# Two copies of the recurrence moved to ScalarE, a new entry, and partial sums of the down projection added by GpSimd's DMAs

## The chip, the cores and the metric

The kernel runs on one core of one Trainium2 chip. The metric is the device time of one execution in microseconds, and lower is better. A run's time is that of the whole program; the profile is of one further execution of the same program.

## What is computed

The input is a sequence of 1024 tokens with 1024 channels. Two blocks follow each other, both in float32. The first has a mixture of three branches (a linear recurrence with a 64x64 state per head, a short convolution and a pooling branch), gates and an output projection. The second has windowed attention and retention, then a gated feed-forward network. Cut to what the change touches:

```python
h = rms_norm(x, pre_norm_w)                       # the entry: 1024 x 1024
p = h @ w_in                                      # r, k, v, gates, fills
y_a = rwkv7_branch(...)                           # the recurrence, chunks of 64 tokens
...
m = rms_norm_2(h, ffn_norm_w)
h = h + (silu(m @ w_gate) * (m @ w_up)) @ w_down  # w_down: 2816 x 1024, the down projection
```

## The kernel before, in words

The channels lie on the 128 partitions and the tokens along the free dimension, 1024 of them in two halves of 512 (one PSUM bank each). Matrix products are made with float32r operands split in two: a tile W becomes Whi (a copy rounded to float32r, made by ScalarE) and Wlo = W - Whi (a subtraction by VectorE or GpSimd), and each product is three matmuls: hi x hi, hi x lo, lo x hi. So TensorE's work stands fixed, and the other engines prepare operands and empty banks.

Each engine runs one long program of its own, written as Python generators ("streams"), and the order in which the streams of an engine are woven is written out by hand in `ORDER`: a letter is a stream, a number behind it how many of its steps. An engine takes its instructions strictly in that order; all dependences between engines are semaphores (`S.<signal>.tick(key)` adds, `wait_ge(*S.<signal>.at(key))` waits). `PICKS` says which PSUM bank each product takes where there is a choice. Every engine operation of the same kind has the line of its small wrapper: 120 matmul, 123 transpose, 126 activation, 129 tensor_tensor, 137 scalar_tensor_tensor, 140 copy, 143 memset, 146 DMA. So the profile is read by tiles.

**The entry** (`begin` and `tokens_in`, `token_norms`, lines 658, 1255, 1288, 1825, 1841). ScalarE's queue loads the gain row `pre_norm_w` into one partition of xn[1]. TensorE first makes 4 products of zeros, then spreads the row over 128 partitions by a product with a row of ones, then makes 8 more products of zeros. ScalarE copies the result, times 32, to `g_row`, and after that squares the tokens of each 128-token tile with a running sum. GpSimd raises the sum to the power -0.5, VectorE makes xn = x * rstd * g_row, TensorE transposes it, ScalarE writes Hhi and VectorE Hlo, and the dense products of `w_in` begin.

**The recurrence** (45 to 700 us; stream "s" is `stage`, "i" `invert`, "c" `chain`, "p" `prep`, "g" `group_norm`, "f" and "e" the other consumers of `w_in`). There are 8 units of 512 tokens and 128 channels, each of 8 chunks and 2 heads. For a unit VectorE inverts 32 small triangular matrices `Nn` by 60 dependent operations ("Ntmp" and "Nn"), adds the diagonal, and copies the transposed first half to `Nt` (lines 2060 to 2064; the profile calls it Nn, line 140). SP writes both to memory and reads them back in other layouts for TensorE. The `WU` tile takes two quarters of transposes out of PSUM: rows 0 to 63 by ScalarE, rows 64 to 127 by VectorE (line 2080). Between the small products of the units stand the dense products of `w_in`, which cover their latency. The chain from chunk to chunk goes TensorE, `Xs` on VectorE, TensorE. ScalarE makes `rk`, squares from which a key's norm is had.

**The down projection** (from 2011 us; `down_products` 857, `down` 1764 and 2507, `block_weights` 1777, 2589, 2794 and 3028, `hidden` 1803, 2549 and 2785). The 22 row tiles of `w_down` are paired, and products of 2x2 blocks are made with seven products in place of eight (Winograd's form). 16 blocks w0 to w15 are made: four pairs of output tiles (dp) times four groups of row pairs; a block takes two or three row pairs, and each of its seven products A11, S3, S4, S2, S1, A12, A22 three matmuls per pair. The 16 accumulators `acc` and 4 `x6` lie in SBUF. In group 0 (w0 to w3) ScalarE copies most products there, in the others VectorE adds each product from PSUM to its accumulator:

```python
    def add(to, out, b, name, point):
        dve.wait_ge(*S.dense_pe.at(("prod", name, b)))
        dve.tt(to[:], banks.of(("st", out, b)), to[:], ALU.add).then_inc(*S.ffn_dve.tick((point, b)))
```

VectorE also forms the sums S1 to S4 of the weight quarters (wSrcS), the low halves of S2 to S4 (wLoS), and the sums and low halves of the hidden side (hT). GpSimd makes the low halves of A11, S1, A12 and A22 (wLoA, wLoS) and of three hidden tiles. SP loads a block's weight quarters (wSrcA) after the low halves of the block before have been made: A11 and A21 after S3, S4 and A11, the others after A22.

## Time and profile before

| | |
|---|---|
| time, median of 3 runs | 2244.04 us (2243.98 to 2244.30) |
| the profiled execution | 2244.64 us |
| its span, first to last instruction | 2242.9 us |
| TensorE, VectorE, ScalarE, GpSimd busy | 2218.5, 1554.3, 837.8, 476.1 us |
| first dense product starts | 14.91 us |
| down projection, first and last product | 2011.3 to 2235.6 us |

The windows view gives the busy time of each engine in a stretch of the span; the waits view sums how long an engine, or TensorE's weight loads (PEld), stood idle and what released it; the chain that ended last is followed back from the last instruction; the timeline lists instructions by their start. A matmul's end is modelled, so that a matmul before a short wait is drawn longer and the wait is partly hidden in it.

### The profile page before, as it was taken

The page shows a single profiled execution, that of the slowest core. Times are in us where ns is not written, and L with a number is a line of the kernel's source. Part 1 is how long each engine was busy: PE and PEld are TensorE (multiplying, and loading weights), DVE is VectorE, ACT ScalarE, POOL GpSimd, SP SyncE. Part 2 cuts the span into 40 slices and gives each one's busy share as a digit, 9 for nine tenths or more (in the row PEclk, how much of TensorE's full clock was granted, in tenths as well). Part 3 has the DMA queues.
Part 4 walks back from the last instruction along what each step waited for, and adds up shares of the span by engine and source line. Part 5 has one row for each costly group of instructions (what it writes and reads, how often), then busy time and mean ns, then how long its engine had stood idle before and what let it go on. Part 6 is the DMA issues. An engine that isn't in the chain of part 4 may idle for free.

```text
span 2242.9 us, 30930 instructions
## 1 busy us (share of the span) xinstructions
PE 2218.5 (99%) x11960; PEld 1835.1 (82%) x11960; DVE 1554.3 (69%) x2646; ACT 837.8 (37%) x1486; POOL 476.1 (21%) x379
## 2 busy tenths in 40 slices
...
GB/s 151 44 57 53 64 58 35 62 56 58 65 113 116 113 113 150 291 169 129 91 72 52 59 38 59 39 127 113 76 85 85 85 78 82 85 115 106 107 122 149
DMA packets 254547, 208.55 MB, mean 93 GB/s; under 512 B 49985, under 2 KB 223681, under 8 KB 254402
## 3 DMA queue, kind: packets, MB, share of 16 engines
...
q14 instruction: 50, 0.41, 0.1%
q10 hardware_dynamic: 2, 0.00, 0.0%
...
## 4 chain that ended last, share of the span: by engine, by line
PE 79%; DVE 14%; issue 2%; DMA 2%; SPq 1%; POOL 1%; ACT 1%; DVEq 0%; POOLq 0%; ACTq 0%
PE PS L120 77%; PE PS L123 3%; DVE Nn L129 2%; DVE Ntmp L129 2%; SPq L146 1%; DVE Wlo L129 1%; DMA Nn<-scr_ns 1%; DVE acc L129 1%; DMA wSrcA<-in_w_down_dram 1%; DVE wSrcS L129 1%; DVE Zt L129 1%; DVE cy L137 1%; DVE ST L137 1%; POOL wLoA L129 0%; DVE Xs L129 0%
## 5 line engine op out<-in xcount | busy, mean ns | idle before, releaser
L120 PE MATMUL PS<-Hhi,Wlo 128*128 128x512 f32 (+1 forms) x1304 | 421.4, 390 | 0.0
L120 PE MATMUL PS<-Hlo,Whi 128*128 128x512 f32 (+1 forms) x1304 | 420.5, 389 | 0.0
L120 PE MATMUL PS<-Hhi,Whi 128*128 128x512 f32 (+1 forms) x1304 | 419.5, 388 | 0.9 <-DVE Hlo L129 0.9
L120 PEld LDWEIGHTS PS<-Hhi,Whi 128*128 128x128 f32 x1304 | 240.3, 189 | 45.9 <-issue 2.0
L120 PEld LDWEIGHTS PS<-Hhi,Wlo 128*128 128x128 f32 x1304 | 239.1, 189 | 45.9 <-issue 2.4
L120 PEld LDWEIGHTS PS<-Hlo,Whi 128*128 128x128 f32 x1304 | 239.6, 189 | 44.9 <-issue 2.2
L126 ACT ACTIVATE Whi<-Wraw 128x512 fp32r<-128x512 f32 x170 | 106.4, 629 | 333.7 <-PE PS L120 333.3
L129 DVE TENSOR_TENSOR Wlo<-Wraw,Whi 128x512 fp32r<-128x512 f32 x166 | 121.4, 734 | 73.2 <-ACT Whi L126 72.4
L129 DVE TENSOR_TENSOR Ntmp<-Nn 32x30 f32<-32x30 f32 (+14 forms) x240 | 76.7, 319 | 23.3 <-DMA Nn<-scr_ns 17.1
L129 POOL TENSOR_TENSOR sm<-sm,expo 128x8 f32<-128x8 f32 x8 | 17.3, 2165 | 340.4 <-DVE sm L134 340.3
L129 DVE TENSOR_TENSOR Nn<-Nn,Ntmp 32x30 f32<-32x30 f32 (+14 forms) x240 | 76.6, 319 | 6.9
L129 DVE TENSOR_TENSOR acc<-PS,acc 128x512 f32<-128x512 f32 x108 | 71.0, 679 | 10.4 <-PE PS L120 10.2
L129 POOL TENSOR_TENSOR Wlo<-wA,Whi 128x512 fp32r<-128x512 f32 x38 | 51.0, 1342 | 110.6 <-ACT Whi L126 110.6
L129 DVE TENSOR_TENSOR wS<-wA,wA 128x512 f32<-128x512 f32 x38 | 26.1, 688 | 57.9 <-DMA wA<-in_w_gate_dram 57.9
L120 PE MATMUL PS<-YMlo,Whi 128*128 128x512 f32 (+1 forms) x188 | 64.7, 372 | 0.0
L120 PE MATMUL PS<-YMhi,Whi 128*128 128x512 f32 (+1 forms) x188 | 64.6, 371 | 0.0
L120 PE MATMUL PS<-YMhi,Wlo 128*128 128x512 f32 (+1 forms) x188 | 64.5, 371 | 0.0
L126 ACT ACTIVATE smx<-smx,small,q_norms 128x385 f32<-128x385 f32 (+1 forms) x64 | 43.1, 675 | 47.7 <-DVE small L137 47.7
L129 POOL TENSOR_TENSOR rsb<-rsb,expo 128x8 f32<-128x8 f32 x8 | 13.2, 1654 | 218.3 <-DVE rsb L133 218.3
L120 PE MATMUL PS<-YMhi,fSlo 128*128 128x512 f32 x152 | 59.1, 389 | 0.0
L120 PE MATMUL PS<-YMlo,fShi 128*128 128x512 f32 x152 | 59.1, 389 | 0.0
L120 PE MATMUL PS<-YMhi,fShi 128*128 128x512 f32 x152 | 59.1, 389 | 0.0
...
## 6 DMA issues: line engine op xcount, KB each, us to landing
Wraw<-in_w_in_dram SPq DMA_DIRECT2D x126, 256.0 KB, 2.9
...
gwA<-in_w_in_dram SPq DMA_DIRECT2D x40, 256.0 KB, 3.4
wA<-in_w_gate_dram SPq DMA_DIRECT2D x38, 256.0 KB, 3.2
wA<-in_w_up_dram SPq DMA_DIRECT2D x38, 256.0 KB, 3.3
...
```

What stands on the lines that cost most here:

```text
L120: return self.h.matmul(out, lhsT, rhs, start=start, stop=stop, skip_group_check=True)
L123: return self.h.transpose(out, in_, ident)
L126: return self.h.activation(out, in_, func, **kw)
L129: return self.h.tensor_tensor(out, a, b, op)
L137: return self.h.scalar_tensor_tensor(out, a, s, b, op0, op1)
L146: return self.h.dma_start(out, in_)
```

## The change

Four things are done.

1. Entry. GpSimd clears the whole tile xn[1] first (a new first step of its stream "q"), ScalarE's queue waits for that and then loads the gain row into its first partition. The row is spread by a product over all 128 partitions with xn[2], whose first row is 32 and whose others are 0. The products of zeros are 5 and 2 in place of 4 and 8. VectorE takes the gain straight from PSUM for the first two token tiles (four operations), and ScalarE copies it to `g_row` only after these; the squares of the first tiles stand before that copy in ScalarE's order.
2. Recurrence. The copy to `Nt` (8) and the copies of rows 64 to 127 of `WU` (16) go from VectorE to ScalarE; SP's write of the transposed inverse and TensorE's product G wait for ScalarE.
3. Down projection. In blocks w4 to w11 the products A12 and A22 are no longer added by VectorE. ScalarE copies each to one of two new tiles `part`, and GpSimd issues a DMA that adds `part` to the accumulator in SBUF (16 DMAs of 256 KB). ScalarE waits for the landing of the one two before; the next add to the same accumulator, GpSimd's or VectorE's, waits for the landing too.
4. Three loads of constants share one semaphore (`side_dma`), `PICKS` and all of `ORDER` are written anew, those of attention too. In GpSimd's order the pair of adds of block w(b) stands after the low half of A11 of w(b+1) and before that of S1.

Of the diff the signal names, the two other waits for `side_dma`, the new `PICKS` and the orders of the other engines are left out:

```diff
--- before.py
+++ after.py
@@ -17,7 +17,7 @@
 NRAW, NSPL = 3, 4
-WARM = (4, 8)
+WARM = (5, 2)
@@ -141,6 +141,9 @@
+
+    def dma_add(self, out, in_):
+        return self.h.dma_start(out, in_, accum_op=ALU.add)
@@ -266,6 +269,8 @@
+
+ADDED = [(b, point) for b in BLOCKS_W[4:-4] for point in ("ca", "cd")]
@@ -531,6 +536,7 @@
         W.wsrc = {name: mw(f"wSrc{name}", [128, 3, 128]) for name in WSRC}
+        self.part = [mw(f"part{i}", [128, HT]) for i in range(2)]
@@ -604,6 +610,11 @@
         return ("prod", "A22", LAST["f"]) if i < 2 else ("tile", ("fu", 21))
+    def added(self, b, point):
+
+        n = ADDED.index((b, point))
+        return (self.S.acc0_dma, self.S.acc1_dma)[n % 2].at(n)
@@ -659,11 +670,11 @@
             pe.mm(SB[3], K.Whi[NSPL - 1][:, 0, :], K.Whi[NSPL - 1][:])
+        pe.wait_ge(*S.start_dve.at("one"))
         pe.wait_ge(*S.grow_dma.at(0))
         for j in range(2):
-            bank, _ = banks.take(("gain", j), (f"SB{j}",), [S.init_act.at("gain")])
-            t = pe.mm(bank, K.xn[0][0:1, 0:128], K.xn[1][0:1, j * 512:j * 512 + 512])
-        t.then_inc(*S.xtr_pe.tick("gain"))
+            bank, _ = banks.take(("gain", j), (f"SB{j}",), [S.init_act.at("gain"), S.xn_dve.at((1, j))])
+            pe.mm(bank, K.xn[2][:, 0:128], K.xn[1][:, j * 512:j * 512 + 512]).then_inc(*S.xtr_pe.tick(("gain", j)))
@@ -858,8 +869,9 @@
         own = S.ffn_act if b[1] < 4 else S.ffn_dve
-        read = {"a": [own.at(("ca", b))], "b": [S.ffn_dve.at(("x6", b))], "c": [S.ffn_dve.at(("cc", b))],
-                "d": [own.at(("cd", b))], "e": [own.at(("g2", b))]}
+        out_by = S.ffn_act if b in BLOCKS_W[:-4] else S.ffn_dve
+        read = {"a": [out_by.at(("ca", b))], "b": [S.ffn_dve.at(("x6", b))], "c": [S.ffn_dve.at(("cc", b))],
+                "d": [out_by.at(("cd", b))], "e": [own.at(("g2", b))]}
@@ -949,7 +961,7 @@
             for g in range(2):
-                bk, before = banks.take(("av", u, g), SIDE, [S.stage_act.at(("a", u, g)), S.stage_dve.at(("v", u, g))])
+                bk, before = banks.take(("av", u, g), SIDE, [S.stage_act.at(("a", u, g))])
@@ -977,7 +989,7 @@
             pe.wait_ge(*S.inv_dve.at(("A", u, 1, 1)))
-            pe.wait_ge(*S.stage_dve.at(("v", u, 1)))
+            pe.wait_ge(*S.stage_act.at(("a", u, 1)))
@@ -1253,11 +1265,13 @@
     def begin():
+        act.wait_ge(*S.xrstd_pool.at("row"))
         act.dma(K.xn[1][0:1, :], K.D["pre_norm_w"]).then_inc(*S.grow_dma.tick(0, by=16))
         yield
-        act.wait_ge(*S.xtr_pe.at("gain"))
+        act.wait_ge(*S.xtr_pe.at(("gain", 1)))
+        act.wait_ge(*S.xn_dve.at((1, 1)))
         for j in range(2):
-            act.act(K.g_row[:, j * 512:j * 512 + 512], banks.of(("gain", j)), ACT.Copy, scale=32.0).then_inc(*S.init_act.tick("gain"))
+            act.act(K.g_row[:, j * 512:j * 512 + 512], banks.of(("gain", j)), ACT.Copy).then_inc(*S.init_act.tick("gain"))
@@ -1411,12 +1425,18 @@
                 act.wait_ge(*S.init_dve.at("wu"))
-                act.act(K.WU[0:64, :, 4 * g:4 * g + 4, 0:64], src[0:64], ACT.Copy).then_inc(*S.stage_act.tick(("a", u, g)))
+                act.act(K.WU[0:64, :, 4 * g:4 * g + 4, 0:64], src[0:64], ACT.Copy).then_inc(*S.stage_act.tick())
+                act.act(K.WU[64:128, :, 4 * g:4 * g + 4, 64:128], src[64:128], ACT.Copy).then_inc(*S.stage_act.tick(("a", u, g)))
...
+            act.wait_ge(*S.inv_dve.at(("dg", u)))
+            if u:
+                act.wait_ge(*S.xtw_dma.at(u - 1))
+            act.act(K.Nt, K.Nn[0:16].rearrange("p s t -> p t s"), ACT.Copy).then_inc(*S.stage_act.tick(("nt", u)))
+            yield
@@ -1773,6 +1793,16 @@
                 yield
+        for n, (b, point) in enumerate(ADDED):
+            if n > 1:
+                act.wait_ge(*K.added(*ADDED[n - 2]))
+            else:
+                for m in K.blocks_done():
+                    act.wait_ge(*m)
+            name, out = {"ca": ("A12", "a"), "cd": ("A22", "d")}[point]
+            act.wait_ge(*S.dense_pe.at(("prod", name, b)))
+            act.act(K.part[n % 2][:], banks.of(("st", out, b)), ACT.Copy).then_inc(*S.ffn_act.tick((point, b)))
+            yield
@@ -1823,9 +1853,11 @@
     def begin():
-        dve.memset(K.xn[0][0:1, 0:128], 1.0).then_inc(*S.start_dve.tick("one"))
         dve.memset(K.xse[:, :, 1024:1025], float(np.sqrt(1024 * EPS))).then_inc(*S.start_dve.tick("eps"))
         dve.memset(K.Whi[NSPL - 1][:].bitcast(F32), 0.0).then_inc(*S.start_dve.tick("zero"))
+        dve.memset(K.xn[2][:, 0:128], 0.0).then_inc(*S.start_dve.tick("rows"))
+        dve.wait_ge(*S.start_dve.at("rows"))
+        dve.memset(K.xn[2][0:1, 0:128], 32.0).then_inc(*S.start_dve.tick("one"))
@@ -1839,13 +1871,17 @@
     def token_norms():
-        dve.wait_ge(*S.init_act.at("gain"))
         for i in range(8):
+            if i == 2:
+                dve.wait_ge(*S.init_act.at("gain"))
...
-                dve.stt(K.xn[i % NXN][:, cols], K.xs[i % NXS][:, cols], K.ss[:, 8 + i:9 + i], K.g_row[:, cols], ALU.mult,
+                gain = banks.of(("gain", keys[0][1])) if i < 2 else K.g_row[:]
+                if i < 2:
+                    dve.wait_ge(*S.xtr_pe.at(("gain", keys[0][1])))
+                dve.stt(K.xn[i % NXN][:, cols], K.xs[i % NXS][:, cols], K.ss[:, 8 + i:9 + i], gain, ALU.mult,
@@ -2057,11 +2093,6 @@
             yield
-            if u:
-                dve.wait_ge(*S.xtw_dma.at(u - 1))
-            dve.wait_ge(*S.inv_dve.last())
-            dve.cp(K.Nt, Nn[0:16].rearrange("p s t -> p t s")).then_inc(*S.inv_dve.tick(("nt", u)))
-            yield
@@ -2072,13 +2103,6 @@
             yield
-            for g in range(2):
-                src = banks.of(("av", u, g)).rearrange("p (c h f) -> p h c f", c=4, h=2)
-                dve.wait_ge(*S.stage_pe.at(("av", u, g)))
-                if u:
-                    dve.wait_ge(*S.stage_pe.at(("de", u - 1, 1, 1)))
-                dve.cp(K.WU[64:128, :, 4 * g:4 * g + 4, 64:128], src[64:128]).then_inc(*S.stage_dve.tick(("v", u, g)))
-                yield
@@ -2529,16 +2553,17 @@
                 dve.wait_ge(*S.ffn_dve.last())
+                dve.wait_ge(*K.added(before, "cd"))
...
-            dve.wait_ge(*own.at(("ca", before)))
-            yield from add(c11, "a", b, "A12", "ca")
-            dve.wait_ge(*own.at(("cd", before)))
-            yield from add(c21, "d", b, "A22", "cd")
+            if (b, "ca") not in ADDED:
+                dve.wait_ge(*K.added(before, "ca"))
+                yield from add(c11, "a", b, "A12", "ca")
+                yield from add(c21, "d", b, "A22", "cd")
@@ -2680,6 +2705,8 @@
     def token_norms():
+        pool.memset(K.xn[1][:], 0.0).then_inc(*S.xrstd_pool.tick("row"))
+        yield
@@ -2801,7 +2828,16 @@
                 yield
-    return {"w": weights(), "q": token_norms(), "p": prep(), "g": group_norm(), "t": projections(), "m": out_weights(),
+    def down():
+        for n, (b, point) in enumerate(ADDED):
+            m = 2 * (b[1] % 4) + (point == "cd")
+            pool.wait_ge(*S.ffn_act.at((point, b)))
+            if b[1] > 7:
+                pool.wait_ge(*K.added(("w", b[1] - 4), point))
+            pool.dma_add(K.acc[m, 0][:], K.part[n % 2][:]).then_inc(*(S.acc0_dma, S.acc1_dma)[n % 2].tick(n, by=16))
+            yield
+
+    return {"D": down(), "w": weights(), "q": token_norms(), "p": prep(), "g": group_norm(), "t": projections(), "m": out_weights(),
@@ -2826,9 +2862,9 @@
         sp.dma(K.cst[:, idc[1]:], D["cst"][:, idc[1]:]).then_inc(*S.cst_dma.tick("rest", by=16))
-        sp.dma(K.wup[:], D["wup"]).then_inc(*S.wup_dma.tick(0, by=16))
-        sp.dma(K.pw[:], D["pool_w"][0].rearrange("g c d -> c g d")).then_inc(*S.pw_dma.tick(0, by=16))
-        sp.dma(K.pf[:], D["pfix"]).then_inc(*S.pf_dma.tick(0, by=16))
+        sp.dma(K.wup[:], D["wup"]).then_inc(*S.side_dma.tick(by=16))
+        sp.dma(K.pw[:], D["pool_w"][0].rearrange("g c d -> c g d")).then_inc(*S.side_dma.tick(by=16))
+        sp.dma(K.pf[:], D["pfix"]).then_inc(*S.side_dma.tick(0, by=16))
@@ -2869,7 +2905,7 @@
             yield
-            sp.wait_ge(*S.inv_dve.at(("nt", u)))
+            sp.wait_ge(*S.stage_act.at(("nt", u)))
...
     "pool":
-        "q2w2q2w2q4p4gp3gpgp4g2p4g2SgS39t8m8n16k4yxzo2rk2yxozxyzxyorkzkxyzoxykzxoryzk2xyozxkyzorkxyzxkyn8S76u"
-        "Wu2W3u2WuW3uWu2W4u3W4u3W4u2W4u2W4u2W4u2W4u3W4u2W4u2W4u2W3uW12",
+        "q3w2q2w2q4p6gp2g2p2gp4gp2g2SgS39t8m8n16k4yxzo2ryxk2zxoyzxyozxrk2yzoxykzxork2yzxyozxkyzokrxykzxyn8S76"
+        "uWu2W3u2WuW2uW2u2W4u3W4u3W4u2D2uW4uDuDuW4D2W4u2D2uW4u2D2uW4uDuDuW4D2W4u2D2uW15",
...
```

## Rows read from the trace of the kernel before

**Rows 1.** The page, part 1: busy time, share of the span and instructions.
```profile
PE 2218.5 (99%) x11960; PEld 1835.1 (82%) x11960; DVE 1554.3 (69%) x2646; ACT 837.8 (37%) x1486; POOL 476.1 (21%) x379
```

**Rows 2.** Windows: start:end, us, busy (instructions) by engine, PEclk, DMA share, GB/s.
```profile
0.00:15.00 15.00, 11.54 (x33) 6.63 (x34) 4.72 (x10) 7.64 (x14) 3.31 (x8) 1.00 0.59 197
45.00:700.00 655.00, 646.44 (x3790) 527.22 (x3789) 499.95 (x1040) 237.43 (x423) 42.17 (x27) 1.00 0.22 63
1150.00:1480.00 330.00, 328.89 (x2407) 275.89 (x2405) 250.76 (x580) 160.74 (x320) 80.22 (x61) 1.00 0.21 55
```

**Rows 3.** Timeline of the entry: start, us, engine, line, what [idle before].
```profile
0.71 0.51 ACTq L146 DMA_DIRECT2D xn<-in_pre_norm_w_dram  x1
...
3.58 3.78 PE L120 MATMUL PS<-xn,xn 1*128 1x512 f32 x4
...
7.29 3.58 PE L120 MATMUL PS<-Whi 128*128 128x512 f32 x8
7.39 1.08 ACT L126 ACTIVATE g_row<-PS 128x512 f32<-128x512 f32 x2 [4.85 <-PE PS L120]
...
11.25 0.63 PE L123 MATMUL PS<-cst,xn 128*128 128x128 f32 x4 [0.38 <-DVE xn L137]
...
14.91 0.36 PE L120 MATMUL PS<-Hhi,Whi 128*128 128x256 f32 x1 [0.89 <-DVE Hlo L129]
```

**Rows 4.** Groups of the first 45 us, and tile xs: its loads.
```profile
L143 DVE MEMSET WU<- 64x1024 f32 x1 | 0.9, 912 | 0.3 <-issue 0.3
...
DMA to landing us min/median/max: 3.6/5.8/8.0
```

**Rows 5.** Groups by form of VectorE and ScalarE, 45 to 720 us.
```profile
L140 DVE COPY WU<-PS 64x512 f32<-64x512 f32 x16 | 11.1, 694 | 5.2 <-PE PS L123 4.8
...
L140 DVE COPY Nn<-Nn 16x1024 f32<-16x1024 f32 x8 | 8.9, 1107 | 0.7
...
L126 ACT ACTIVATE WU<-PS 64x512 f32<-64x512 f32 x64 | 37.9, 592 | 34.1 <-PE PS L120 17.3 <-PE PS L123 15.9
```

**Rows 6.** Waits of the weight loads, then the products, 45 to 700: us, times, longest.
```profile
PEld PS L120 <- DVE Xs L129: 12.1, 21, 1.1
PEld PS L120 <- ACT rk L126: 3.4, 3, 1.5
...
PE PS L120 <- DVE Xs L129: 2.5, 6, 0.7
PE PS L120 <- ACT rk L126: 2.2, 3, 1.1
```

**Rows 7.** The chain that ended last, cut to 45 to 700 us: start, us, what.
```profile
121.33 1.11 DVE Nn L140
...
154.84 0.69 DVE WU L140
```

**Rows 8.** Windows: blocks w4 to w11 of the down projection, and w5.
```profile
2062.81:2179.80 116.99, 115.70 (x506) 94.16 (x504) 108.71 (x164) 48.50 (x98) 68.09 (x50) 1.00 0.36 108
2077.96:2092.24 14.28, 14.28 (x65) 11.82 (x63) 13.54 (x20) 4.32 (x10) 8.52 (x6) 1.00 0.41 126
```

**Rows 9.** Waits of the weight loads, then the products, in these blocks.
```profile
PEld PS L120 <- DVE wLoS L129: 2.9, 4, 1.0
...
PE PS L120 <- DVE wLoS L129: 1.2, 3, 0.6
```

**Rows 10.** Groups by form, 2045 to 2215 us.
```profile
L129 DVE TENSOR_TENSOR acc<-PS,acc 128x512 f32<-128x512 f32 x82 | 54.1, 679 | 7.1 <-PE PS L120 6.9
...
L129 POOL TENSOR_TENSOR wLoA<-wSrcA,wHiA 128x384 fp32r<-128x384 f32 x32 | 39.9, 1269 | 4.8 <-ACT wHiA L126 4.8
```

**Rows 11.** Timeline of GpSimd in w5 and w6.
```profile
2081.97 2.15 POOL L129 TENSOR_TENSOR wLoS<-wSrcS,wHiS 128x384 fp32r<-128x384 f32 x1 [4.57 <-ACT wHiS L126]
...
2097.38 1.51 POOL L129 TENSOR_TENSOR wLoS<-wSrcS,wHiS 128x384 fp32r<-128x384 f32 x1 [6.20 <-ACT wHiS L126]
```

**Rows 12.** DMA issues: tiles, queue, count, KB each, median us to landing.
```profile
hB11raw<-scr_fb SPq DMA_DIRECT2D x11, 256.0 KB, 3.0
```

More of the change, by code:

```diff
@@ new lines @@
+        "scsd3csdscd2s2cd3pdcd4cd3cd3cd9pd8pd8gd13id5pd16id6s2d4sd5s2d3s2d3scsd2cds2dcd2s2cd3pdcd3pdcd3cd3pcd"
+        "25id12id5gpd5sd3sdsd5s2d3s2d3scsd2cds2dcd2s2cd3pdcd4cd3cd3cd24gd19pd3sd2sd2pd2sd6s2d3s2d2pd2csdcd3cs"
+        "dcd3cd3cd3cd3cd9sd2sd2sd3sd5id6id4pd4pd8pgd19id61pd8id5m2d2sdsd3sd5s2d3s2d3scsd2cds2cd3cs2dcd2pd2cd6"
+        "cd6pcd7pd15gd6id7pd16id6s2d4sd5s2d3s2d2m2cdsdcds2dcd2scsd2csd2cpd4pcd3cd3pd29id23m2d4gpd7sdsd3sd5id4"
+        "sdsd2sdsdmd2mcsdcd2scsd3cs2d2csd3cd4cd5cd22gd35s2d4sd6s2d3s2d3scsd2cd3cd3cd3cd3cd3cd3cd42gd688n2d16n"
```

111 lines of the change are left out of this document (53 added, 58 removed).

## The prediction

> **What bounds the kernel now.** I read the page first: TensorE is busy 2218.5 of 2242.9 us [rows 1], so at most 24.4 us are idle. The windows by stage come next [rows 2]: the first 15 us hold 3.5 us of idle, the recurrence (45 to 700 us) 8.6, attention 1.1. VectorE is busy 500 of 655 us in the recurrence and 108.7 of 117.0 in the middle of the down projection [rows 8]; there work taken off it can matter. Busy is not the whole loss, since a product whose successor waits is drawn long. The waits view shows the rest: in the recurrence TensorE and its weight loads wait 12.1 + 2.5 = 14.6 us for VectorE's Xs and 3.4 + 2.2 = 5.6 us for ScalarE's rk [rows 6]. In the down projection the yardstick is one block of three pairs without a wait, 14.28 us; the eight blocks w4 to w11 took 117.0 [rows 8] against 8 x 14.28 = 114.2, a loss of 2.8 us. What they waited for is the low half of the sum S4, 2.9 + 1.2 us, out of VectorE's queue [rows 9].
>
> **Part 1, the entry.** Today: the gain row's DMA goes out at 0.71, its product starts at 3.58, the copies to g_row end at 8.47 (7.39 + 1.08), behind them stand the squares of token 0, then GpSimd's power and xn; transposes at 11.25, first dense product at 14.91 [rows 3]. After the change the gain DMA waits until GpSimd has cleared a 128x1024 row. No row has that. VectorE's clearing of 64x1024 took 0.91 [rows 4]; I take 0.9, between nearly nothing and twice that. So the DMA goes out at about 1.3, the product starts 2.87 later as now, at 4.2, takes the same 3.8 us (its 512 columns stay) and ends at 8.0; two idle products of 0.45 follow (8 took 3.58), and transposes may start at 8.9. The squares no longer stand behind g_row: token 0's load lands 3.6 us after issue at the earliest [rows 4], at 4.3, so xn(0) can come by 6.8, as soon as the first half of the gain is in PSUM. Transposes thus start at 9.0 to 9.5, about 2 us earlier. Of the 3.66 us from there to the dense product one weight conversion on ScalarE goes, and a third square comes in, whose load lands in the crowd of the first loads: nothing for the two together. **-2.2 us** (0 to -3.5). The idle products run at 0.45 us for 512 columns, the level of 1.2 GHz; 63 products of a block in 14.28 us are 0.227 each, 2.4 GHz. Should the new start, broken by a gap, leave TensorE at the lower level for its first 24 steps of 0.12, that gives back 3 us; the upper end of this part is +0.8.
>
> **Part 2, the recurrence.** Off VectorE: 16 WU copies (11.1 us) and 8 Nn copies (8.9), 20.0 of its 500 us [rows 5]. Onto ScalarE: 16 x 0.59 = 9.4 and, taking its copy as long as VectorE's, 8 x 1.1 = 8.9; 18.3 us on an engine busy 237 of 655. In the chain of waits, cut to 45 to 700 us, 4 Nn copies and 12 WU copies stand on the path (the first of each in [rows 7]): 4 x 1.1 + 12 x 0.69 = 12.7 us, the most that the part can give straight away. It can also lose: ScalarE takes its steps in order, and where its queue stands waiting for the inversion, its own rk is late, for which TensorE waits 5.6 us already; double that is the other end. Between -12.7 and +5.6 I take **-5 us**, nearest to the direct measure: a third of the 14.6 us that TensorE waits for Xs, behind copies in the same queue. SP's write of the inverse now waits for ScalarE; behind it on SP stand weight loads, whose buffers are three deep. The bank of the WU transposes comes free after two ScalarE copies in a row (1.2 us) instead of two side by side (0.7): 0.5 us twice a unit, under the dense steps between.
>
> **Part 3, the down projection.** Off VectorE in w4 to w11: 16 adds of 0.68 = 10.9 us [rows 10], 1.4 a block. ScalarE gets 16 copies of 0.59, at 48.5 of 117 us busy. GpSimd gets 16 DMA issues. No row has one: ScalarE's queue took 0.51 us for its transfer [rows 3], GpSimd's own subtraction of 128x384 takes 1.27 [rows 10]; I take 1.3, by the engine that must do the work, and 0.3 to 3 as bounds. Each pair stands in its order just after the low half of A11 and before that of S1. There GpSimd is idle today for 4.6 and 6.2 us in two successive blocks [rows 11], so 2.6 us are hidden. Queued behind the pair are the low halves of S1, A12 and A22; behind A22's wait SP's next weight loads, and behind those VectorE's S sums. The landing (3.0 us for 256 KB from SP's queue [rows 12]; I allow 8) has a block's 14.3 us before its buffer is wanted, and four blocks before its sum is. With 1.4 us a block off the queue that makes S4, of the 2.8 us lost I take back **-2.0 us** (-2.8 to +1).
> A rule speaks against this part. The trace: GpSimd's subtraction of S1 stands directly behind the idle stretch, so there is room of 4.6 to 6.2 us [rows 11] and no issue yet to time. The Trainium skill, SBUF — State Buffer, warns in its section SBUF: two separate sides that descriptors written by GpSimd are starved while VectorE copies in its two-port modes, with an example of 0.62 us that became 3.1. By that a pair would cost 6.2 us and the -2.0 would be about 0. The page names copies, and VectorE's work here is additions and subtractions; no row here shows either.
>
> **Part 4, the rest.** Three constants share one semaphore; all are there long before the recurrence uses them: 0. All orders are written anew, attention's too, where no operation changes and TensorE idles 1.1 us: between -1 and +2, I take 0. The tail keeps its last steps: 0.
>
> **Sum.** -2.2 - 5.0 - 2.0 = -9.2. The profiled execution took 2244.64 us, span 2242.9 and 1.7 around it; 2235.4 for it, and as it lies 0.6 above the median of the runs, **2234.8**.
>
> **Rivals.**
> A, ScalarE takes VectorE's place (0.14). For it: 8.9 us of Nn copies in a queue taken in order, whose rk TensorE waits for. Against: it idles 64% of the recurrence. -5 becomes +1: 2240.8.
> B, the copies were hidden (0.11). For it: VectorE idles 24% there, and half of the Nn copies are not on the chain. -5 becomes 0, and of the down projection half remains: 2240.8 as well, with less in the waits for rk.
> C, slower: GpSimd's DMA issue becomes the bound of the down projection (0.13). A pair has 6.2 us; from 3.1 us an issue on it overruns. At 4 us it is late by 1.8, the low half of A22, the next loads and the S sums with it, in 8 blocks: 14 us, and the -2.0 is gone: 2251. Against: no operation of GpSimd of this size takes that long [rows 10].
> D, more (0.16): the recurrence gives what stands on its chain, 12.7 us: 2227.
> E, the orders or the start lose what the parts give (0.04): 2246.
>
> **Numbers.** The forecast's own case has 0.42, with 2229 to 2240. About 0.2%, 4.5 us, is what a measurement of this kernel can tell from no change, so faster means below 2239.5. Of the forecast 0.39, D 0.16, A and B 0.08: 0.63. Same: 0.03 and 0.17 of these, 0.02 of C: 0.22. Slower: C 0.11, E 0.04: 0.15. The range, 2226 to 2250, leaves out the half of D that goes below its price and C from 4 us an issue up.
>
> **What would show it.** Right: the first dense product at 12 to 13.5 us; waits for Xs below 14.6 us, with those for rk not above 5.6; w4 to w11 in 115 us; a DMA issue of GpSimd under 2 us. Wrong: GpSimd's subtraction of S1 later against its block's start, and weight loads with it (C); waits for rk or WU grown by several us (A); the first product late or its steps twice as long; a loss in attention, where I expect nothing.

## The result, and the profile after

The changed kernel took 2256.51 us (median of 5 runs, 2255.40 to 2259.08) against 2244.04 before (2243.50 to 2246.02): a ratio of 1.0059, 95% interval 1.0048 to 1.0070. It is 12.5 us slower; 9.2 us faster was forecast, and the range ended at 2250.

The page, part 1, of the changed kernel:

```profile
PE 2219.0 (98%) x11955; PEld 1833.0 (81%) x11955; DVE 1517.5 (67%) x2607; ACT 873.5 (39%) x1526; POOL 500.8 (22%) x396
```

Beside [rows 1] VectorE lost 36.8 us of work, ScalarE gained 35.7 and GpSimd 24.7. TensorE's busy time is the same, its span 12.1 us longer. So the work was moved as the change says, and the loss is waiting. Where it lies is read from the first product of each stage, which is the same instruction in both kernels: here the timeline of TensorE, first of the kernel before, then of the changed one, at the first product of the fills' squared weights (behind the recurrence), of attention, of the feed-forward network and of the down projection (start us, us, what).

```profile
699.75 0.39 PE L120 MATMUL PS<-Hhi,gShi 128*128 128x512 f32 x1
...
1138.53 0.28 PE L120 MATMUL PS<-cst,rot 128*128 128x2 f32 x2
...
1581.55 0.39 PE L120 MATMUL PS<-YMhi,Whi 128*128 128x512 f32 x1
...
2011.29 0.39 PE L120 MATMUL PS<-hB11hi,wHiA 128*128 128x512 f32 x1
```

```profile
691.17 0.39 PE L120 MATMUL PS<-Hhi,gShi 128*128 128x512 f32 x1
...
1129.91 0.28 PE L120 MATMUL PS<-cst,rot 128*128 128x2 f32 x2
...
1579.52 0.39 PE L120 MATMUL PS<-YMhi,Whi 128*128 128x512 f32 x1
...
2009.27 0.39 PE L120 MATMUL PS<-hB11hi,wHiA 128*128 128x512 f32 x1
```

The changed kernel is 8.6 us ahead behind the recurrence and 8.6 ahead at attention; at the feed-forward network it is 2.0 ahead, and 2.0 at the down projection. So attention lost 6.6 us. The last product of the down projection starts at 2246.6 against 2235.2, 11.4 behind, so the down projection lost 13.4 us, and the tail 0.7. These make the 12.1 us of the span: -2.05 for the entry (below), -6.5 for the recurrence, +6.6 for attention, +13.4 and +0.7. Of the 13.4 us, the blocks w0 to w3 gave 2.1 back, w4 to w11 cost 12.0 and w12 to w15 3.5.

Windows of the changed kernel, as in [rows 2] and [rows 8] (the last row is w4 to w11, from its first product to w12's):

```profile
0.00:15.00 15.00, 10.55 (x41) 6.69 (x42) 6.47 (x13) 9.81 (x17) 5.94 (x11) 1.00 0.90 309
...
45.00:700.00 655.00, 650.96 (x3819) 532.33 (x3819) 479.83 (x1018) 268.60 (x450) 54.01 (x29) 1.00 0.23 65
...
1150.00:1480.00 330.00, 324.29 (x2376) 271.11 (x2375) 247.12 (x576) 160.09 (x318) 78.80 (x60) 1.00 0.21 56
```

```profile
2058.71:2187.71 129.00, 119.57 (x506) 94.51 (x504) 109.47 (x155) 58.06 (x115) 79.35 (x66) 0.99 0.49 127
```

The recurrence's idle fell from 8.6 to 4.0 us. Attention's rose from 1.1 to 5.7. The blocks w4 to w11 took 129.0 us where they had taken 117.0. VectorE is busy 109.5 us in them although it was given 16 sums fewer.

**The entry**, in the timeline of the changed kernel, as in [rows 3]:

```profile
0.73 0.95 POOL L143 MEMSET xn<- 128x1024 f32 x1 [0.29 <-POOLq L3350]
...
1.71 0.50 ACTq L149 DMA_DIRECT2D xn<-in_pre_norm_w_dram  x1
...
5.37 3.69 PE L120 MATMUL PS<-xn,xn 128*128 128x512 f32 x4 [1.39 <-DMA xn<-in_pre_norm_w_dram]
...
9.37 0.60 PE L123 MATMUL PS<-cst,xn 128*128 128x128 f32 x4
...
12.15 1.09 ACT L126 ACTIVATE g_row<-PS 128x512 f32<-128x512 f32 x2 [0.30 <-DVE xn L137]
...
12.86 0.36 PE L120 MATMUL PS<-Hhi,Whi 128*128 128x256 f32 x1 [0.69 <-DVE Hlo L129]
```

Clearing the row took 0.95 us; the gain's DMA went out at 1.71 and its product started 3.7 us later, not 2.9. The squares no longer stand behind g_row, the transposes start at 9.37, and the first dense product at 12.86, 2.05 us earlier. The record gives a granted clock of 1.00 for this stretch, the upper level, in both kernels; the products of zeros nevertheless start 0.43 us apart in both (here at 2.07, 2.50, 2.92 and 3.35), the pace that a granted clock of 0.50 shows further down, and the dense products 0.12 us apart. So in this trace the reserve for a start at the lower level was not needed. It was in two of the seven profiled kernels with the new entry: entry_rec_only has a granted clock of 0.50 from 14.1 to 17.5 us and after_S4_first from 13.4 to 16.8, and their first 24 dense products took 5.9 and 5.8 us in place of 4.3, which is 1.5 us each.

**The recurrence.** Waits of the weight loads, then of the products, 45 to 700 us, as in [rows 6], and two groups of ScalarE, as in [rows 5]:

```profile
PEld PS L120 <- DVE Xs L129: 6.2, 17, 0.6
...
PEld PS L120 <- ACT rk L126: 1.2, 2, 0.7
```

```profile
PE PS L120 <- ACT rk L126: 0.4, 2, 0.3
PE PS L120 <- DVE Xs L129: 0.3, 2, 0.2
```

```profile
L126 ACT ACTIVATE WU<-PS 64x512 f32<-64x512 f32 x80 | 47.4, 593 | 31.2 <-PE PS L123 15.8 <-PE PS L120 14.1
...
L126 ACT ACTIVATE Nn<-Nn 16x1024 f32<-16x1024 f32 x8 | 16.7, 2083 | 25.1 <-DVE Nn L133 25.1
```

The waits for Xs fell from 14.6 to 6.5 us and those for rk, of which the prediction was afraid, from 5.6 to 1.6. The copy to Nt takes ScalarE 2.08 us, where VectorE took 1.11; the path still got shorter.

**The down projection.** Waits of the weight loads in w4 to w11, as in [rows 9], and the groups of GpSimd's adds and ScalarE's copies:

```profile
PEld PS L120 <- DVE wLoS L129: 8.3, 9, 2.0
PEld PS L120 <- ACT wHiS L126: 4.8, 4, 1.7
```

```profile
L146 POOL DMA_DIRECT2D acc<-part x16 | 14.5, 906 | 17.6 <-ACT part L126 17.6
...
L126 ACT ACTIVATE part<-PS 128x512 f32<-128x512 f32 x16 | 9.6, 598 | 21.3 <-PE PS L120 21.2
```

An issue costs 0.91 us, less than the 1.3 taken. The waits for VectorE's low halves of the sums grew from 2.9 to 8.3 us, and those for ScalarE's high halves from 0.5 to 4.8. The stalls of w4 (1.6 and 1.7 us) are followed by 3.4 us at a granted clock of 0.50, its lower level, with 9 products where 3.4 us at the upper level hold 15 of the pitch of 0.227. The kernel before has one such stretch in these blocks, behind a stall of 2.0 us in w3; the changed kernel has a second one in w12. A stall thus costs more than its length: at half the clock a stretch loses half of its own, here 1.7 us. The first two lines are of the changed kernel, the third of the kernel before:

```profile
2067.10:2070.50 3.40, 3.40 (x9) 2.63 (x9) 2.85 (x3) 0.46 (x1) 3.40 (x4) 0.50 0.07 22
2207.05:2210.45 3.40, 3.33 (x8) 2.13 (x8) 2.02 (x3) 0.52 (x1) 0.76 (x1) 0.50 0.70 198
```

```profile
2051.70:2055.10 3.40, 3.40 (x10) 2.64 (x9) 1.44 (x2) 1.31 (x4) 3.27 (x3) 0.50 0.23 66
```

### The profile page after: what moved, and what is told of

Read it like the earlier page. It is cut to its first block, busy times and chain, and to the rows that moved or that the text cites. A ratio compares the mean times of both kernels' runs of the same rounds, so it can differ in the third digit from the quotient of the medians.

```text
span 2255.0 us, 30936 instructions
## 1 busy us (share of the span) xinstructions
PE 2219.0 (98%) x11955; PEld 1833.0 (81%) x11955; DVE 1517.5 (67%) x2607; ACT 873.5 (39%) x1526; POOL 500.8 (22%) x396
## 4 chain that ended last, share of the span: by engine, by line
PE 80%; DVE 13%; DMA 2%; issue 2%; POOL 1%; SPq 1%; ACT 1%; DVEq 0%; ACTq 0%; POOLq 0%
PE PS L120 77%; PE PS L123 3%; DVE Ntmp L129 2%; DVE Nn L129 2%; DMA wSrcA<-in_w_down_dram 1%; SPq L149 1%; DVE Wlo L129 1%; DVE Zt L129 1%; DVE acc L129 1%; POOL sm L129 1%; DVE wSrcS L129 1%; DVE ST L137 0%; DVE Xs L129 0%; DVE wLoS L129 0%; DVE cy L137 0%
## 5 line engine op out<-in xcount | busy, mean ns | idle before, releaser
L129 DVE TENSOR_TENSOR Ntmp<-Nn 32x30 f32<-32x30 f32 (+14 forms) x240 | 76.3, 318 | 19.4 <-DMA Nn<-scr_ns 13.6
L129 DVE TENSOR_TENSOR acc<-PS,acc 128x512 f32<-128x512 f32 x92 | 61.5, 682 | 17.7 <-PE PS L120 17.4
L126 ACT ACTIVATE WU<-PS 64x512 f32<-64x512 f32 x80 | 47.4, 593 | 31.2 <-PE PS L123 15.8
```

What stands on the lines that cost most here:

```text
L126: return self.h.activation(out, in_, func, **kw)
L129: return self.h.tensor_tensor(out, a, b, op)
```

## The experiments

They were run in six groups, each beside runs of the kernel before on the same chip; its medians there were 2242.95, 2242.59, 2242.79, 2245.54, 2243.62 and 2242.84. "Orders" are the strings in `ORDER`; the four stages can be joined from the two kernels, since between them the counts of all streams agree.

### Which stage loses

**down_alone**: the kernel before with part 3.

```diff
@@ ORDER, "pool", from the down projection on @@
-"uWu2W3u2WuW3uWu2W4u3W4u3W4u2W4u2W4u2W4u2W4u3W4u2W4u2W4u2W3uW12"
+"uWu2W3u2WuW2uW2u2W4u3W4u3W4u2D2uW4uDuDuW4D2W4u2D2uW4u2D2uW4uDuDuW4D2W4u2D2uW15"
...
+    return {"D": down(), "w": weights(), "q": token_norms(), "p": prep(), "g": group_norm(), "t": projections(), "m": out_weights(),
```

> Only part 3: the kernel before with the changed down projection, its code and its orders. Theory 1 (each stage's loss is its own, and the traces of before and after can be read stage by stage): the down projection took 224.3 us to its last product before and 237.7 after, and the last stretch 0.7 us more, so this kernel is 14 us slower than before, 2258. Rival (the loss comes from an interplay with the earlier start or the new entry and recurrence): clearly less, under 2250.

2258.81, ratio 1.0075 (1.0060 to 1.0090), 15.9 us slower.

**after_old_down**: the changed kernel with the down projection's code and orders of before.

```diff
-ADDED = [(b, point) for b in BLOCKS_W[4:-4] for point in ("ca", "cd")]
...
-            if (b, "ca") not in ADDED:
-                dve.wait_ge(*K.added(before, "ca"))
-                yield from add(c11, "a", b, "A12", "ca")
-                yield from add(c21, "d", b, "A22", "cd")
+            dve.wait_ge(*own.at(("ca", before)))
+            yield from add(c11, "a", b, "A12", "ca")
+            dve.wait_ge(*own.at(("cd", before)))
+            yield from add(c21, "d", b, "A22", "cd")
```

> The changed kernel with the down projection of before, code and orders. Theory 1: it keeps the 2.0 us that the changed kernel was ahead where the down projection began (2011.29 against 2009.27), so 2242. Rival: 2256 as changed, or anything over 2246, if the stages do not add.

2240.43, ratio 0.9991 (0.9982 to 1.0001).

**after_old_attention**: the changed kernel with the attention part of the five orders and of `PICKS` of before; GpSimd's shows the size of it.

```diff
@@ ORDER, "pool", attention @@
-"k4yxzo2ryxk2zxoyzxyozxrk2yzoxykzxork2yzxyozxkyzokrxykzxyn"
+"k4yxzo2rk2yxozxyzxyorkzkxyzoxykzxoryzk2xyozxkyzorkxyzxkyn"
```

> The changed kernel with the attention order of before in all five queues; no operation is added or removed. Theory 1: the changed kernel was 8.6 us ahead where attention began and 2.0 where it ended, so the new order alone costs 6.6 us and this comes to 2250. Rival (attention lost because the earlier stages left it other times of arrival, for which the old order would be as bad): 2256, no better than the changed kernel.

2253.48, ratio 1.0047 (1.0032 to 1.0062). That lies between the two forecasts, 2250 and 2256. In its trace attention took nearly what it took before (1129.7 to 1574.3, 444.5 us, against 443.0; 449.6 in the changed kernel). Of these 5.1 us, 3.0 were given back behind it: in the down projection, its tail left out, the granted clock was 0.50 for 13.7 us in place of 6.8 (w6 and w10 lost 9.5 us in place of 6.4).

**entry_rec_only**: the changed kernel with both.

```diff
@@ what is left of the change @@
 WARM = (5, 2)
...
+                act.act(K.WU[64:128, :, 4 * g:4 * g + 4, 64:128], src[64:128], ACT.Copy).then_inc(*S.stage_act.tick(("a", u, g)))
...
+            act.act(K.Nt, K.Nn[0:16].rearrange("p s t -> p t s"), ACT.Copy).then_inc(*S.stage_act.tick(("nt", u)))
```

> Parts 1 and 2 alone: the new entry and the recurrence copies on ScalarE, with attention and down projection as before. Theory 1: 8.6 us faster than before, 2235.4, 0.9962 of before. Rival: the gain is eaten by the old orders behind it, 2242 or more.

2235.44, ratio 0.9967 (0.9955 to 0.9979): faster than both kernels. The stages add to within 2 or 3 us: parts 1 and 2 give 7.5 us, the orders of attention cost 5.0 (2240.43 - 2235.44, one chip, and 6.6 in the trace), part 3 costs 15.9 by itself and 18.0 (2253.48 - 2235.44) on top of parts 1 and 2. The first three make 13.4 us, and the changed kernel measured 12.5.

### What of part 3 loses: the sums or the orders

**new_order_old_sums**: the new orders, VectorE adds all products itself (orders of w5 to w7 shown).

```diff
@@ ORDER, "dve", from S3 of w5 on, beside down_alone @@
-"WH2W2DWDWH2W2D2HDHDH2DWDHW2HWHWDHW2DHD4W3DW2DW2DHDH2D"
+"WH2W2DWD2WH2W2D3HDHDH2DWD2HW2HWHWD2HW2DHD5W3D2W2DW2DHDH2D"
@@ ORDER, "pool": no D; "act": no D of w4 to w11 @@
```

> The kernel before with the new orders of the down projection alone: VectorE adds all the products itself as before (the two sums of each block w4 to w11 put back right behind the sum of S1 and ahead of the next block's first sum), no part tiles, no copies, no DMA adds. Theory O (the new orders lose the time, by themselves): close to the part 3 kernel, 2252 to 2260. Theory M (the moved sums lose it: GpSimd's two issues a block, or ScalarE's copies that wait for the product): 2241 to 2246.

2257.20, ratio 1.0064 (1.0049 to 1.0079). The orders alone, `PICKS` included, cost 14.6 us. In its trace the granted clock is 0.50 for 10.2 us of w4 to w12, 3.4 in w4 and 6.8 in w10, which at half the clock costs 5.1 us, where the kernel before lost 1.7 us in this way, in w3; each time a stall of TensorE came first.

**old_order_new_sums**: the orders of before, only the sums moved.

```diff
@@ ORDER, "pool", down projection, beside the kernel before @@
-"uWu2W3u2WuW3uWu2W4u3W4u3W4u2W4u2W4u2W4u2W4u3W4u2W4u2W4u2W3uW12"
+"uWu2W3u2WuW3uWu2W4u3W4u3W4u2D2W4u2D2W4u2D2W4u2D2W4u3D2W4u2D2W4u2D2W4u2D2W3uW12"
```

> The kernel before with its own orders, and only the two sums of w4 to w11 moved: ScalarE's two copies stand right behind the high part of S3 of the next block, GpSimd's two DMA adds directly ahead of the low half of S1 of the next block, VectorE's two sums are taken out. Theory O: 2241 to 2244, which is what the prediction gave for part 3 (-2.0). Theory M: 2252 or more.

2250.39, ratio 1.0032 (1.0019 to 1.0045), between the two. Its blocks tell more: w5 to w8 lose nothing, where they lost 1.6 us before, as the prediction had it. From w9 on it loses: w9 to w11 3.6 us (0.3 before) and w12 5.2 (1.8). There single operations of VectorE take up to 5.4 us. The time lies in neither forecast (2241 to 2244 and 2252 or more): the orders and the moved sums each lose.

**no_gpsimd_adds**: down_alone without the adds.

```diff
-            pool.dma_add(K.acc[m, 0][:], K.part[n % 2][:]).then_inc(*(S.acc0_dma, S.acc1_dma)[n % 2].tick(n, by=16))
...
-                act.wait_ge(*K.added(*ADDED[n - 2]))
...
-                dve.wait_ge(*K.added(before, "ca"))
```

> The part 3 kernel (2258.8) without GpSimd's 16 DMA adds and without every wait for them; ScalarE still copies the products to the part tiles, and these sums are left out of the output. If GpSimd's queue (0.9 us an issue, and its waits for ScalarE) or the traffic of the adds loses the time: 2248 or less. Theory O, or ScalarE's copies: at most 2 us faster, 2256 to 2259.

2256.37, ratio 1.0060 (1.0045 to 1.0075): 2.4 us off. In the new orders GpSimd's adds are not the main loss; what they cost lies in w12, which lost 1.7 us in place of 4.8. Nor is any operation of VectorE held long there: the longest takes 2.3 us in the changed kernel and 2.4 in down_alone.

**part_copies_later**: down_alone with ScalarE's copies behind the high half of S3.

```diff
@@ ORDER, "act", from w4 on, beside down_alone @@
-"W5HWH5DWDW5H2WH2DH2DWHW5HWD2W6HWH3DWHDHW5H2WH2DHWHDHW5H2WH2DH2DHW6HWDWDW6H4WDHDHW5HW21"
+"W5HWH5WD2W5H2WH4WD2HW5HW2D2W5HWH3WD2H2W5H2WH3WD2H2W5H2WH5WD2W5HW2D2W6H4WD2H2W5HW21"
```

> The part 3 kernel with ScalarE's two copies of a block moved behind the high part of S3 of the next block, in place of ahead of it; nothing else changes. If the copies' wait for the products holds up the high parts behind them (S3's came at 14.1 to 15.3 us of its block or in the next one, at 11.8 to 14.3 before): 3 to 8 us faster than 2258.8. Theory O or GpSimd's queue: within 2 us of it.

2262.09, ratio 1.0088 (1.0071 to 1.0105). It is 3.3 us slower than down_alone, outside both forecasts, and TensorE's products wait 7.0 us for the high halves in w4 to w11, where they waited 5.1. So the copies' waits ahead of the high half of S3 are not what holds the high halves up.

### What holds VectorE off in the old orders

**old_order_no_adds**: as no_gpsimd_adds, from old_order_new_sums.

```diff
@@ ORDER, "pool", beside old_order_new_sums @@
-"...W4u3W4u3W4u2D2W4u2D2W4u2D2W4u2D2W4u3D2W4u2D2W4u2D2W4u2D2W3uW12"
+"...W4u3W4u3W4u2W4u2W4u2W4u2W4u3W4u2W4u2W4u2W3uW12"
```

> The kernel old_order_new_sums (2250.4) without GpSimd's 16 DMA adds and the waits for them; these sums are left out of the output. There three subtractions of VectorE in w9 to w11 took 5.4, 5.3 and 4.7 us, each begun while GpSimd issued an add and went straight on to four low halves. Theory L (an issue with low halves directly behind it holds VectorE off): none over 2 us here, and 2240 to 2243. Rival (four low halves in a row hold it off by themselves, or ScalarE's copies lose the time): the long ones stay, 2247 or more.

2243.00, ratio 0.9999 (0.9989 to 1.0008). Theory L holds, since no operation of VectorE takes over 1.8 us, though the time shows no gain: w5 to w11 lose nothing, and w13 loses 5.1 in place of 3.9, which was not settled. The two kernels side by side, the same operations of w9. First old_order_new_sums, VectorE and then GpSimd in the timeline:

```profile
2139.20 5.40 DVE L129 TENSOR_TENSOR hT3lo<-hT3raw,hT3hi 128x512 fp32r<-128x512 f32 x1
```

```profile
2138.34 1.77 POOL L146 DMA_DIRECT2D acc<-part  x2
2139.50 1.65 POOL L129 TENSOR_TENSOR wLoS<-wSrcS,wHiS 128x384 fp32r<-128x384 f32 x1
2140.48 3.56 POOL L129 TENSOR_TENSOR wLoA<-wSrcA,wHiA 128x384 fp32r<-128x384 f32 x3
```

Then old_order_no_adds:

```profile
2138.93 1.50 DVE L129 TENSOR_TENSOR hT3lo<-hT3raw,hT3hi 128x512 fp32r<-128x512 f32 x1
```

```profile
2138.48 1.40 POOL L129 TENSOR_TENSOR wLoS<-wSrcS,wHiS 128x384 fp32r<-128x384 f32 x1 [0.36 <-ACT wHiS L126]
2139.84 4.32 POOL L129 TENSOR_TENSOR wLoA<-wSrcA,wHiA 128x384 fp32r<-128x384 f32 x3
```

Without an issue ahead of them, GpSimd's four low halves follow each other at 1.4 us and VectorE works in between, at 1.5 us for this subtraction. Behind two issues they follow at 1.0 us, and VectorE's subtraction, begun during the second issue, ends only 0.6 us after the last of the four: 5.4 us. In w10 and w11 it is 5.3 and 4.7. In w11 the subtraction began at 2173.93, 0.4 us into the first of the four low halves, so it need not begin while an issue runs.

**old_order_adds_earlier**: the adds of w8 to w11 one step earlier.

```diff
@@ ORDER, "pool", beside old_order_new_sums @@
-"...W4u2D2W4u2D2W4u2D2W4u2D2W4u3D2W4u2D2W4u2D2W4u2D2W3uW12"
+"...W4u2D2W4u2D2W4u2D2W4u2D2W4u2D2uW4uD2uW4uD2uW4uD2uW3uW12"
```

> The kernel old_order_new_sums with the two adds of w8 to w11 one step earlier in GpSimd's order, ahead of the last low half of a hidden tile, so that GpSimd idles between an add and the low halves of the weights, as it did in w5 to w8, where nothing was lost. Theory L: 2240 to 2243, w4 to w11 in 115.5 us. Rival (w9 to w12 lose for another reason, the landing of the adds or the sums they hold up): 2247 or more.

2246.72, ratio 1.0018 (1.0008 to 1.0027). The time misses theory L's 2240 to 2243 and just misses its rival's 2247. In the trace the blocks w5 to w11 now lose nothing and w4 0.3 (2.7 for the eight before): that is what theory L said of them, and a gain of 2.4 us where the prediction's part 3 had 2.0. But w12 loses 5.3 (1.8 before), and w13 5.1 (3.9 before). In w12 an issue still stands ahead of hB22lo, VectorE's subtraction beside them takes 2.35 us, and SP's four loads of weights, behind eight loads for the output, take up to 2.9 us each to issue (0.4 to 0.8 before).

**entry_rec_adds_earlier**: the same orders in entry_rec_only.

```diff
@@ ORDER, "act", down projection, beside entry_rec_only: D2 behind S3 of the next block @@
-"W5H2WH3WH2W6H2WHW5H3WH2W6HWH3WH2W6H2WH3W5H2WHWHW6H5W6H2WH3WH2W5HW21"
+"W5H2WH3WD2H2W6H2WD2HW5H3WH2WD2W5HWH3WD2H2W6H2WD2H3W5H2WHWD2HW6H5WD2W5H2WH3WD2H2W5HW21"
```

> Parts 1 and 2 (2235.4 alone) together with the moved sums in the old order with the earlier adds. Theory L: 1 to 3 us faster than parts 1 and 2 alone, 2232 to 2235. Rival: 2240 or more, as the moved sums lost 7.8 us in the old order.

2236.49, ratio 0.9973 (0.9962 to 0.9985): no better than entry_rec_only's 0.9967, and not the 2232 to 2235 of theory L. Moving the sums gained nothing in any order that was tried.

### What the new orders of the down projection lose

**others_new_order**: new_order_old_sums with GpSimd's order of before.

```diff
@@ ORDER, "pool", beside new_order_old_sums @@
-"uWu2W3u2WuW2uW2u2W4u3W4u3W4u3W4u3W8u3W4u3W4u3W8u3W15"
+"uWu2W3u2WuW3uWu2W4u3W4u3W4u2W4u2W4u2W4u2W4u3W4u2W4u2W4u2W3uW12"
```

> The kernel new_order_old_sums (2257.2, orders new, sums on VectorE as before) with GpSimd's order of the down projection as before, so that the low half of a hidden tile B21 stands behind those of the weights again where it stood so. Theory P (GpSimd's place for hB21lo loses the time: it waits there for VectorE's difference, and the low halves of S1, A12 and A22, the next loads and the S3 sum are late behind it): 2241 to 2249. If the loss lies in VectorE's, ScalarE's or SP's order: 2253 or more.

2256.51, ratio 1.0056 (1.0040 to 1.0073). Theory P falls. The orders of ScalarE, SP and TensorE were not put back by themselves.

**new_order_S4_first** and **after_S4_first**: VectorE's sums and low halves of the weights ahead of the hidden steps between them, in w4 to w12.

```diff
@@ ORDER, "dve", w5 to w7, beside new_order_old_sums @@
-"WH2W2DWD2WH2W2D3HDHDH2DWD2HW2HWHWD2HW2DHD5W3D2W2DW2DHDH2D"
+"WH2W6D3H2D3HDHDH2DWD2HW6H2D2HDHD5W7D4HDH2D"
```

> The kernel new_order_old_sums (2257.2) with one regrouping of VectorE's order in w4 to w12: behind the low half of S3 come at once the sums S1, S2, S4 and the low halves of S4 and S2, and then what stood between them (low halves of the hidden T2 and T1, the difference T4, the sums x1 and u2); in ScalarE's order hT4hi of w4 goes behind the high half of A22. Theory S (VectorE's steps of a hidden tile and its sums ahead of S4's low half lose the time): 2243 to 2249, TensorE's waits for S4's low half (9.1 us) below 3. Rival (the loss is spread over the order in other ways, as ScalarE's and SP's): 2254 or more.

> The changed kernel (2256.5) with the same regrouping and nothing else. Theory S: 2243 to 2250. If the adds of GpSimd then lose what the order gave back (VectorE held off behind an issue, as in old_order_new_sums): 2250 to 2255, with single operations of VectorE over 2.5 us in w5 to w12. Rival: 2255 or more with the waits at S4 as they are.

2260.12 (1.0066, 1.0051 to 1.0081) and 2259.22 (1.0070, 1.0053 to 1.0086). Theory S falls: the wait only moved. TensorE's products in w4 to w11, first in new_order_old_sums, then in new_order_S4_first:

```profile
PE PS L120 <- DVE wLoS L129: 6.0, 6, 1.6
PE PS L120 <- ACT wHiS L126: 3.9, 4, 1.9
```

```profile
PE PS L120 <- POOL wLoS L129: 6.2, 5, 1.9
PE PS L120 <- ACT wHiS L126: 4.1, 10, 0.7
PE PS L120 <- DVE wLoS L129: 2.3, 3, 1.0
```

VectorE's difference T4 comes later, by 1.2 us in w5 and 2.3 in w6, so does GpSimd's hB21lo, and the low half of S1 behind it.

**S4_first_gpsimd_old** and **after_S4_first_gpsimd_old**: both edits at once; the cut shows the first of the two.

```diff
@@ ORDER, "dve", w5 to w7, and "pool", beside new_order_old_sums @@
-"WH2W2DWD2WH2W2D3HDHDH2DWD2HW2HWHWD2HW2DHD5W3D2W2DW2DHDH2D"
+"WH2W6D3H2D3HDHDH2DWD2HW6H2D2HDHD5W7D4HDH2D"
-"uWu2W3u2WuW2uW2u2W4u3W4u3W4u3W4u3W8u3W4u3W4u3W8u3W15"
+"uWu2W3u2WuW3uWu2W4u3W4u3W4u2W4u2W4u2W4u2W4u3W4u2W4u2W4u2W3uW12"
```

> The kernel new_order_S4_first (VectorE's sums as before, S4's low half ahead of the hidden steps) and besides GpSimd's order of before, where hB21lo mostly stands behind the low halves of S1, A12 and A22. Each of the two alone gave nothing (2260.1 and 2256.5). Theory Q (the two places hold each other: the hidden tile's steps are either ahead of S4's low half on VectorE or, through T4 and hB21lo, ahead of S1's on GpSimd): 2243 to 2250, neither wait over 3 us. Rival (the loss is elsewhere, in ScalarE's or SP's order): 2254 or more.

> The changed kernel with both of these, and GpSimd's adds in the earlier places. Theory Q: 2241 to 2248 (it keeps the 2.0 us that it is ahead where the down projection begins). Rival: 2254 or more.

2256.48 (1.0055, 1.0040 to 1.0070) and 2262.70 (1.0083, 1.0066 to 1.0099). Theory Q falls as well. In the second of them VectorE was held off again: in w11 and w12 GpSimd issues an add and goes straight on to four subtractions, and a low half of S4 or S2 (128x384) that VectorE begins 0.1 to 0.4 us into the first of them takes 4.5 and 4.8 us; these two blocks lose 3.9 and 8.2 us. What no regrouping within a block can change is the load of a block. Windows from VectorE's S3 sum of a block to that of the next, for w5, w7, w8 and w9 (columns as in [rows 2]; VectorE's busy time is the third after the length). The kernel before:

```profile
2075.68:2089.97 14.29, 14.29 (x64) 11.82 (x63) 13.55 (x22) 6.08 (x13) 8.61 (x7) 1.00 0.37 111
2105.22:2119.81 14.59, 14.26 (x63) 11.46 (x62) 12.97 (x20) 4.25 (x9) 6.67 (x6) 1.00 0.39 109
2119.81:2133.61 13.80, 13.80 (x63) 11.42 (x62) 13.59 (x23) 6.61 (x14) 7.49 (x6) 1.00 0.47 152
2133.61:2148.26 14.65, 14.65 (x67) 12.12 (x66) 12.32 (x23) 6.51 (x13) 10.15 (x7) 1.00 0.36 109
```

new_order_old_sums:

```profile
2076.16:2094.01 17.85, 17.85 (x80) 14.80 (x79) 16.28 (x25) 6.67 (x15) 8.54 (x7) 1.00 0.29 89
2110.39:2124.66 14.27, 13.75 (x60) 10.77 (x59) 10.42 (x18) 5.40 (x11) 6.89 (x6) 1.00 0.36 110
2124.66:2141.25 16.59, 15.20 (x67) 11.94 (x66) 16.59 (x24) 6.66 (x15) 8.88 (x7) 1.00 0.39 127
2141.25:2158.07 16.82, 15.84 (x70) 12.64 (x69) 16.82 (x26) 8.20 (x17) 11.03 (x8) 1.00 0.31 94
```

In w8 and w9 VectorE is never idle, and they take 16.6 and 16.8 us where TensorE's block needs 14.28; in w7 it is idle for 3.9. Before, these stretches hold 6, 4, 6 and 6 of VectorE's eight steps on a hidden tile, in the new orders 8, 3, 8 and 8. Busy time is not work alone: a step takes 0.68 us by itself and up to 1.8 while GpSimd works. In w9 the six steps took 4.6 us before and the eight take 8.1.

**new_order_thin_hidden** and, as control, **before_thin_hidden**: most of these steps on half their columns.

```diff
-                dve.tt(to[:], x[:], y[:], ALU.subtract).then_inc(*done.tick((step, i)))
+                n = HT // 2 if i > 3 else HT
+                dve.tt(to[:, 0:n], x[:, 0:n], y[:, 0:n], ALU.subtract).then_inc(*done.tick((step, i)))
```

> The kernel new_order_old_sums (2257.2) with VectorE's steps of the hidden tiles 4 to 10 on half their columns (T1, T2, T3, T4 and the low halves of T1, T2, T4), the other half being left out of the computation; order, waits and every other step stay. Theory R (VectorE's load in the blocks that get a whole tile, 16.4 to 16.9 us against 14.3, loses the time): the blocks w5 to w11, which lost 12.7 us, lose under 4, and the time is 2243 to 2250. Rival (the places in the queues lose it, whatever the steps cost): over 8 us lost there, 2252 or more.

> The control: the same thinner steps in the kernel before, the same halves left out. Its blocks w5 to w11 lost 1.9 us, so at most 3 us are to be had (w4 and w12 included): 2240 to 2243 by theory R and by its rival.

2249.42 (1.0026, 1.0015 to 1.0037) and 2242.15 (0.9998, 0.9989 to 1.0008). Of the 14.6 us, 7.8 come back, and only 0.7 in the control. The blocks w5 to w11 lose 6.7 us in place of 12.7, w8 and w9 nothing. The time lies in theory R's range, the loss of the blocks between what it and its rival gave. Part of what came back is clock: a granted clock of 0.50 lasts 3.4 us in w4 to w12 in place of 10.2. And a thinner step also brings forward all that stands behind it in VectorE's queue, so that load and place are not told apart by this run. What is left lies mostly in w4 (2.8) and w10 (4.8), at the two halves of S4, and was not settled.

## Why the prediction was wrong, step by step

- **Part 1, the entry**: right. -2.05 measured in the trace, -2.2 taken; the transposes at 9.37 within the 9.0 to 9.5 given. The gain's DMA went out 0.4 us and its product 1.2 us later than worked out, and the transposes still kept their time. The fear of a start at the lower clock was put at 3 us; it came in two other kernels and cost 1.5.
- **Part 2, the recurrence**: right. -6.5 in the trace, -5 taken, and rival A's sign, longer waits for rk, did not come. The term mis-sized is the copy to Nt, 2.08 us and not 1.1: 16.7 us of ScalarE for 8.9, in an engine with room. Together parts 1 and 2 gave 7.5 us by themselves (entry_rec_only), 7.2 being forecast.
- **Part 4, the rest**: this step failed: "no operation changes and TensorE idles 1.1 us: between -1 and +2, I take 0". The new order of attention lost 6.6 us in the trace and 5.0 between two timed kernels. That little is idle bounds what an order can gain; it bounds no loss. In the trace of the changed kernel TensorE's products meet three waits there of 1.1 to 2.0 us (for the softmax's smx, for qx and for a normalisation), where the longest was 0.4. Which steps of the new order bring them about, no run tells; that cause stays open.

```profile
PE PS L123 <- DVE smx L133: 2.0, 1, 2.0
PE PS L123 <- ACT qx L126: 1.3, 1, 1.3
PE PS L123 <- DVE small L2341: 1.1, 1, 1.1
```

- **Part 3, the down projection**: this step failed too, in two places: -2.0 was taken, +13.4 measured in the trace and +15.9 with part 3 alone. The sum of the moved work was right as far as it went: in the old orders w5 to w8 lost nothing, and with the adds in earlier places the eight blocks gave 2.4 us of the 2.8. But the prediction priced the moved sums only and not the order around them, which is as new as attention's. That order was put at nothing without a reason; it costs 14.6 us alone, and about half of it went with thinner steps on the hidden tiles: whole tiles fall to single blocks, in which VectorE is busy 16.3 to 16.8 us for 14.3. That this load is the cause of the half is the likeliest reading and not shown apart from the steps' places; the other half stays open. VectorE's share over w4 to w11, [rows 8], hides the bunching: 92.9% before is 12.3 to 13.6 us in the stretches shown above, which leaves 0.7 to 2.0 us, where two steps more take 1.8 at the 0.92 that a step on a hidden tile took on average. Second, the issues of GpSimd cost 0.91 us and were rightly bounded, but what they do to VectorE was not among the costs. That cost shows in the old orders (old_order_new_sums, 7.8 us slower than before) and not in the changed kernel.
- **Rival C** had the side and nearly the size (2251, and 14 us from the down projection), and the wrong mechanism: an issue does not come near the 3.1 us from which it was to decide, and without any issue the new orders are slow all the same (no_gpsimd_adds, 2.4 us less of 15.9).
- **The rule weighed in part 3.** The traces show no issue starved: 0.91 us on average, beside VectorE's subtractions too. They show the reverse, VectorE held for 4.5 to 5.4 us behind GpSimd in five places of two kernels (old_order_new_sums and after_S4_first_gpsimd_old). The Trainium skill, SBUF — State Buffer, section SBUF: two separate sides, has this side as well: it calls the ports that the two engines share an exclusive lock, which an operation of GpSimd holds for its whole length against one of VectorE with two inputs in SBUF. By that rule, the trace agrees in kind: VectorE's sums with an operand in PSUM stay at 0.68 us throughout, and its subtractions in SBUF stretch. It goes beyond the rule in length, as the hold here lasts through four instructions of GpSimd.
- **The chances**: 0.63 for faster rested on the sum of parts 1 to 3. Rival E, the orders, had 0.04, for a cause that cost some 20 us (14.6 and 5.0). Its price, 2246, lies within the 4.5 us that the prediction itself calls no change, and yet it was counted as slower.
